# The compressed branch's softmax on ScalarE head by head, and one head in four of the full-length branch weighed by VectorE

## What is computed

```python
s = jnp.einsum('bqgrd,bngd->bgrqn', q, kc) * scale + tbl[:, :, t5_bucket(dist)]
p_cmp = masked_softmax(s, dist >= 0)            # compressed branch: at most 63 columns
...
p = masked_softmax(s, (dist >= 0)[:, :, None])  # selected blocks: with 1024 tokens, all 16 blocks
...
p = masked_softmax(s, mask)                     # sliding window of 512
...
return gates[:, :, 0] * o_cmp + gates[:, :, 1] * o_slc + gates[:, :, 2] * o_win
```

## Time and profile before

| | us |
|---|---|
| median of 3 runs | 1511.42 (1508.46 to 1513.57) |
| the profiled execution | 1514.9 |
| its span, first to last instruction | 1513.1 |
| PE busy | 1422.4 (94%) |
| DVE busy | 792.3 (52%) |
| ACT busy | 488.1 (32%) |
| POOL busy | 452.5 (30%) |

### The profile page before, as it was taken

How to read it: one execution, slowest core, us unless ns; L and a number is a source line. 1 busy time by engine, 2 the same in 40 slices (tenths; PEclk the granted TensorE clock), 3 DMA queues, 4 the chain that set the end, 5 groups by cost and what they waited for, 6 DMA issues and landing times.

```text
span 1513.1 us, 22442 instructions
## 1 busy us (share of the span) xinstructions
PE 1422.4 (94%) x8759; PEld 1330.7 (88%) x8759; DVE 792.3 (52%) x1541; ACT 488.1 (32%) x984; POOL 452.5 (30%) x453
## 2 busy tenths in 40 slices
PE   6999999888788888899999999999999999999997
PEld 6999988656566666699999999999999999999996
DVE  5489933226889997522433343435243434435257
ACT  5122124236776776422321121111112111112123
POOL 1113201466888889134210001010101101010105
PEclk9999999999999999899999999999999999999998
DMA  7731114943111102133110202112020202021112
GB/s 201 190 69 42 46 31 125 288 115 88 43 28 29 27 3 43 29 85 99 56 42 18 71 23 66 44 41 72 16 74 15 74 18 67 26 62 50 35 49 115
DMA packets 165817, 99.00 MB, mean 65 GB/s; under 512 B 35650, under 2 KB 160537, under 8 KB 165633
## 3 DMA queue, kind: packets, MB, share of 16 engines
q1 hardware_dynamic: 163217, 88.71, 21.4%
q0 software_dynamic: 2496, 8.88, 2.2%
HBM read 78.33 MB, written 13.19 MB: 60 GB/s over the span
## 4 chain that ended last, share of the span: by engine, by line
PE 78%; DVE 11%; ACT 4%; issue 4%; DMA 1%; SPq 1%; POOL 0%; POOLq 0%; DVEq 0%; ACTq 0%
PE psA L1077 16%; PE psB L1077 16%; PE psC L1077 16%; PE psA L790 4%; PE psB L790 4%; PE psC L790 4%; PE psC L739 3%; DVE small L1835 2%; PE psA L1106 2%; DVE probL L1886 2%; PE psB L1106 2%; PE psC L1106 2%; PE psD L739 1%; DVE ybuf L1670 1%; ACT probH L1324 1%
## 5 line engine op out<-in xcount | busy, mean ns | idle before, releaser
L2224 POOL TENSOR_TENSOR hid<-hid,rstdB 128x352 f32<-128x352 f32 x66 | 74.8, 1164 | 628.9 <-ACT hid L1507 628.9
L1446 ACT CAST wH<-wraw 128x1024 fp32r<-128x1024 f32 (+1 forms) x132 | 86.8, 658 | 259.7 <-PE psC L1077 178.0
L1904 DVE TENSOR_TENSOR wL<-wraw,wH 128x1024 fp32r<-128x1024 f32 (+1 forms) x132 | 107.2, 813 | 37.3 <-ACT wH L1446 37.2
L2201 POOL TENSOR_SCALAR wide<-wide,small 128x128 f32<-128x128 f32 (+7 forms) x64 | 109.3, 1725 | 24.0 <-DVE small L1878 23.8
L1077 PE MATMUL psA<-gH,wH 128*128 128x352 f32 x352 | 113.9, 324 | 0.1
L1077 PE MATMUL psB<-gH,wH 128*128 128x352 f32 x352 | 113.7, 323 | 0.0
L1077 PE MATMUL psC<-gH,wH 128*128 128x352 f32 x352 | 113.5, 322 | 0.0
L1077 PE MATMUL psA<-gH,wL 128*128 128x352 f32 x352 | 113.0, 321 | 0.0
L1077 PE MATMUL psA<-gL,wH 128*128 128x352 f32 x352 | 112.9, 321 | 0.0
L1077 PE MATMUL psB<-gH,wL 128*128 128x352 f32 x352 | 112.9, 321 | 0.0
L1077 PE MATMUL psC<-gL,wH 128*128 128x352 f32 x352 | 112.9, 321 | 0.0
(11 more groups left out here) (430 smaller groups left out, 4120.6 us busy)
## 6 DMA issues: line engine op xcount, KB each, us to landing
wraw<-in_w_gu SPq DMA_DIRECT2D x44, 512.0 KB
wraw<-in_w_down SPq DMA_DIRECT2D x80, 128.0 KB
zraw<-in_w_in SPq DMA_DIRECT2D x12, 512.0 KB
xa<-in_x_prompt SPq DMA_DIRECT2D x8, 512.0 KB, 8.7
pages<-in_cache_cmp_kv SPq DMA_DIRECT2D x32, 128.0 KB, 2.5
qS<-qH SPq DMA_DIRECT2D x32, 128.0 KB, 2.4
qS<-qL SPq DMA_DIRECT2D x32, 128.0 KB, 2.4
xs<-in_x_prompt SPq DMA_DIRECT2D x8, 512.0 KB, 3.8
```

What stands on the lines that cost most here:

```text
L1446: sc_.copy(wH[:, par, 0:nk, :], wraw[:, par, 0:nk, :]).then_inc(s["wH_done"], 1)
L1904: dve.tensor_tensor(wL[:, par, 0:nk, :], wraw[:, par, 0:nk, :], wH[:, par, 0:nk, :].bitcast(F32), ALU.subtract).then_inc(s["wL_done"], 1)
L2201: pool.tensor_scalar(p, p, precs[q % 4][:, r:r + 1], None, ALU.mult).then_inc(s["scaled"], 1)
L2224: pool.tensor_tensor(hid[:, n, :], hid[:, n, :], rstdB[:, c0:c0 + cw], ALU.mult).then_inc(s["up_scaled"], 1)
```

## The change

In the compressed branch VectorE no longer subtracts the maximum: it only reduces it (negated, into `cmax`). ScalarE makes eight exponentials in place of one, each with that head's `cmax` column as bias and its sum into a column of `csum`. VectorE forms 1/sum times gate (`c_weights`), and ScalarE multiplies the eight heads by their weights with eight copies (`c_scale`, now in ScalarE's program, at step (q+1, 1), ahead of the tiles of that step).

In the full-length branch (br 1) head 3 of each group is multiplied by its weight on VectorE (`weigh_head`), at step (q+2, 0), behind that step's bias and maximum, and GpSimd leaves it out. TensorE waits for both counts. Three semaphores are gone: `tri_in` is merged into `posr_in`, `gain2_in` into `gain_in`.

```diff
@@ module
+def weighed(q):
+
+    by_dve = sum(DG.index(n) <= q for n, _ in BY_DVE)
+    return GQ * (q + 1) - by_dve, by_dve
+
+BY_DVE = [(n, GQ - 1) for n in DG if GROUPS[n][2] == 1]
@@ semaphores and loads
-            sp.dma_start(tri[:, :], A["c_tri"]).then_inc(s["tri_in"], 16)
+            sp.dma_start(tri[:, :], A["c_tri"]).then_inc(s["posr_in"], 16)
...
-                        sp.dma_start(gain2[:, :], A["norm2"][0].rearrange("(k p) -> p k", p=P)).then_inc(s["gain2_in"], 16)
+                        sp.dma_start(gain2[:, :], A["norm2"][0].rearrange("(k p) -> p k", p=P)).then_inc(s["gain_in"], 16)
...
-            pe.wait_ge(s["posr_in"], 64)
+            pe.wait_ge(s["posr_in"], 80)
@@ TensorE
-                            pe.wait_ge(s["scaled"], GQ * (DENSE[n] + 1))
+                            pe.wait_ge(s["scaled"], weighed(DENSE[n])[0])
+                            pe.wait_ge(s["scaled_d"], weighed(DENSE[n])[1])
@@ ScalarE
-                    sc_.activation(pcmp[:, :, :, 0:w].rearrange("p r g n -> p (r g) n"),
-                                   p_scores(n, r).rearrange("p (x n) -> p x n", n=HD)[:, :, 0:w], ACT.Exp
-                                   ).then_inc(s["exp_done"], 1)
+                    for r_ in range(GQ):
+                        for g in range(KVH):
+                            k = KVH * r_ + g
+                            op = sc_.activation(pcmp[:, r_, g, 0:w], p_scores(n, r)[:, HD * k:HD * k + w], ACT.Exp,
+                                                bias=cmax[:, k:k + 1], accum_out=csum[:, k:k + 1])
+                    op.then_inc(s["exp_done"], 1)
...
+            def c_scale(n):
+
+                i, w = GROUPS[n][0], g_width(n)
+                sc_.wait_ge(s["cmp_rec"], i + 1)
+                for r in range(GQ):
+                    for g in range(KVH):
+                        k = KVH * r + g
+                        op = sc_.activation(pcmp[:, r, g, 0:w], pcmp[:, r, g, 0:w], ACT.Copy, scale=crec[:, k:k + 1])
+                op.then_inc(s["cmp_scaled"], 1)
...
-            for _, _, jobs, tiles in steps():
+            for q, r, jobs, tiles in steps():
...
+                if r == 1 and q and rider(q - 1) is not None:
+                    c_scale(rider(q - 1))
@@ VectorE
-                link2(dve.tensor_reduce(cmax, flat, AX, ALU.max, negate=True))
-                dve.tensor_tensor(flat, flat, cmax[:, :, None].to_broadcast([P, 2 * GQ, w]), ALU.add).then_inc(s["score_in"], 1)
-
-            def c_scale(n):
-
-                i, w = GROUPS[n][0], g_width(n)
-                flat = pcmp[:, :, :, 0:w].rearrange("p r g n -> p (r g) n")
+                dve.tensor_reduce(cmax, flat, AX, ALU.max, negate=True).then_inc(s["score_in"], 1)
+
+            def c_weights(n):
+
+                i = GROUPS[n][0]
                 dve.wait_ge(s["exp_done"], NSJ + LASTJOB[n] + 1)
-                link2(dve.tensor_reduce(csum, flat, AX, ALU.add))
+                if i:
+                    dve.wait_ge(s["cmp_scaled"], i)
                 link2(dve.reciprocal(crec, csum))
...
-                link2(dve.tensor_tensor(rg, rg, gate, ALU.mult))
-                dve.tensor_tensor(flat, flat, crec[:, :, None].to_broadcast([P, 2 * GQ, w]), ALU.mult
-                                  ).then_inc(s["cmp_scaled"], 1)
+                dve.tensor_tensor(rg, rg, gate, ALU.mult).then_inc(s["cmp_rec"], 1)
...
+            def weigh_head(n, r):
+
+                p = prob(n, r)[:, 0:g_width(n)]
+                dve.tensor_scalar(p, p, precs[DENSE[n] % 4][:, r:r + 1], None, ALU.mult).then_inc(s["scaled_d"], 1)
...
                     if head == 0:
                         group_weights(DG[old])
+                    if (DG[old], head) in BY_DVE:
+                        weigh_head(DG[old], head)
                 if r == 3 and rider(q) is not None:
-                    c_scale(rider(q))
+                    c_weights(rider(q))
@@ GpSimd
                 for r in range(GQ):
+                    if (n, r) in BY_DVE:
+                        continue
                     p = prob(n, r)[:, 0:g_width(n)]
                     pool.tensor_scalar(p, p, precs[q % 4][:, r:r + 1], None, ALU.mult).then_inc(s["scaled"], 1)
```

More of the change, by code:

```diff
@@ L452, in build @@
             "const_in pack_in table_in table4_in gain_in x_in0 x_in1 x_in2 x_in3 x_in4 x_in5 x_in6 x_in7 x_in8 state_in z_in0 z_in1 z_in2 chan_in poolw_in "
-            "tri_in table_mm table_ev stab_mm stab_ev fvec_ev fvec_out btab_in tsel_done prep "
+            "table_mm table_ev stab_mm stab_ev fvec_ev fvec_out btab_in tsel_done prep "
             "sq_done ms_done rstd_done xn_done turn_x evac_xa evac_xd state_turn state_ev "
@@ L458, in build @@
             "late_zero turn_fill turn_drain page_in0 page_in1 page_in2 page_in3 cmpw_in0 cmpw_in1 cmpw_in2 cmpw_used cmp_half cmp_sum cmp_ev posr_in "
-            "gate_mm gate_ev qbd_done score_mm score_in exp_done sum_read cmp_scaled turn_drain_d probT_used keys_used out_done rec_done scaled pl_done o_half o_ev v_pad split_done k_in q_in0 q_in1 q_in2 prob_zero "
+            "gate_mm gate_ev qbd_done score_mm score_in exp_done sum_read cmp_rec cmp_scaled turn_drain_d probT_used keys_used out_done rec_done scaled scaled_d pl_done o_half o_ev v_pad split_done k_in q_in0 q_in1 q_in2 prob_zero "
             "x2_in0 x2_in1 x_pad mixH_done mixL_done raw_in0 raw_in1 wH_done wL_done unit_mm third_mm out_ev rest_ev "
-            "acc_done moment_mm sd_done inv_done t_done silu_done up_scaled hid_done aH_done aL_done y_add gain2_in "
+            "acc_done moment_mm sd_done inv_done t_done silu_done up_scaled hid_done aH_done aL_done y_add "
             "lraw_in0 lraw_in1 lH_done lL_done last_mm y_last back_turn x_add sq_y accf_done ms3 rstd3 y_done_d y_done_a y_out").split()
@@ L707, in load_gu @@
                     sp.wait_ge(s["rest_ev"], 3 * KD)
-                    sp.dma_start(gB[:, :], A["final_norm"][None, :].to_broadcast([P, D])).then_inc(s["gain2_in"], 16)
+                    sp.dma_start(gB[:, :], A["final_norm"][None, :].to_broadcast([P, D])).then_inc(s["gain_in"], 16)
                 for x in range(2 * FT):
@@ L1479, in _ @@
                     sc_.wait_ge(s["mixL_done"], KD)
-                    sc_.wait_ge(s["gain2_in"], 16)
+                    sc_.wait_ge(s["gain_in"], 32)
                 for n, (at, w) in enumerate(tchunks):
@@ L1779, in _ @@
             dve.wait_ge(s["btab_in"], 16)
-            dve.wait_ge(s["tri_in"], 16)
+            dve.wait_ge(s["posr_in"], 80)
             def biased_max(job, sc, w, adds):
@@ L1873, in group_weights @@
                 if q >= 4:
-                    dve.wait_ge(s["scaled"], GQ * (q - 3))
+                    dve.wait_ge(s["scaled"], weighed(q - 4)[0])
+                    dve.wait_ge(s["scaled_d"], weighed(q - 4)[1])
                 dve.reciprocal(rc, psums[q % 4]).then_inc(s["sum_read"], 1)
@@ L1933, in _ @@
                                   ).then_inc(s["mixL_done"], 1)
-            dve.wait_ge(s["gain2_in"], 16)
+            dve.wait_ge(s["gain_in"], 32)
             for m in range(KD):
@@ L2025, in last_scale @@
                                       ).then_inc(s["y_done_d"], 1)
-            dve.wait_ge(s["gain2_in"], 32)
+            dve.wait_ge(s["gain_in"], 48)
             for q, turns in last_steps():
@@ L2189, in out_sum @@
                 u = 2 * i + g
-                pool.wait_ge(s["scaled"], GQ * min(2 * u + 6, len(DG)))
+                pool.wait_ge(s["scaled"], weighed(min(2 * u + 6, len(DG)) - 1)[0])
                 pool.wait_ge(s["o_half"], u + 1)
```

## The result

Median of 14 runs each: 1517.47 us after (1515.03 to 1520.93) against 1513.19 before (1508.46 to 1515.55). The ratio is 1.0033, with a 95% interval of 1.0022 to 1.0043: by it the change makes the kernel slower by 5.0 us (3.3 to 6.5); the two medians alone lie 4.3 us apart. The forecast said slower, by 11 us.

A forecast was written before the change was run, and what follows sets the result against it. VectorE was taken to set the pace in the prompt's attention, ScalarE close behind. Bursts +12.5, sum and scaling -6.7, weighings +6.9, GpSimd holds +1.5 gave +14.2 us; less a fifth, +11: 1522 us, range 1508 to 1534.

The forecast's parts named there:

- The bursts in early tiles: Tiles 0 to 3: ScalarE's added exponentials and copies delay the casts VectorE needs, costing VectorE 7.6 us.
- The bursts in late tiles: Tiles 4 to 7: the same runs of ScalarE exponentials and copies make VectorE late by 4.9 us.
- What leaves VectorE: Compressed branch: sum and scaling gone, 6.7 us saved; the subtraction's 3.0 us taken into the bursts instead.
- The weighings: Full-length branch: sixteen in-place multiplications of one head by its weight, new on VectorE, costing 6.9 us.
- a fifth: Taken off the summed +14.2 us, as a late VectorE waits less at its next wait; leaves +11 us.
- Held by GpSimd: VectorE's new weighings wait for running GpSimd instructions: 3.5 us left in 8 of 15 groups, 1.5 counted.
- The signs that were to be seen: Attention, 353 to 593 us: expected changes in ScalarE's busy time, VectorE's cast waits, GpSimd's weighings and the last maximum.
- absorbed: Rival, attention: VectorE catches up the bursts fully, only its own account counts: -1.3 us, 1510; chance 0.22.
- faster: Rival, attention: weighings and exponentials fall into VectorE's waits: -6.7 us, 1505; chance 0.11; faster as an outcome 0.13.
- within: Outcome for the whole kernel: change of no more than about 0.3% (4.5 us), given 0.26.
- The tail: After the last score at 593 us: set by w_out's transfer, then transposes and casts; after 622 us shifted as a whole.
- ring of three engines: Attention: TensorE's scores, VectorE's maximum, ScalarE's exponential, transpose, ScalarE's cast, VectorE's rest; added ScalarE work can reach VectorE.

The follow-up runs named there:

- E1: The whole change without VectorE's weighings (GpSimd weighs all heads again), timed against the kernel before: ratio 1.0021, +3.2 us.
- E2: The kernel before with only the weighing of head 3 of each full-length group moved to VectorE: ratio 1.0018, +2.7 us.
- E11: The kernel before with two idle one-column copies added on VectorE behind each of the 128 maxima: ratio 1.0063, +9.5 us.
- E10: The kernel before with one idle one-column copy added on ScalarE behind each of the 128 full-length exponentials: ratio 1.0011, +1.7 us.
- E6: The whole change for query tiles 4 to 7 only, the rest as in the kernel before: ratio 0.9987 against it, -2.0 us.
- E12: The kernel before with only the eight exponentials and their sums on ScalarE, in tiles 4 to 7; VectorE scales, GpSimd weighs all: ratio 0.9993, -1.1 us.
- E8: The whole change with ScalarE's eight copies per tile spread as four pairs over four steps: ratio 1.0032 against the kernel before, +4.8 us.

## Why the prediction was right in sign and too large

**The bursts in early tiles: right in sum.** The forecast had 7.6 us for tiles 0 to 3. E1's early stretch grew by 6.3 us while VectorE shed 3.4. What that shed time is worth isn't measured beside the bursts: nothing, if it goes as with the weighings there, or 1.7 at the half that E2 and E11 show without them. So the bursts cost 6.3 to 8.0 us (an estimate from these traces). At tile 2 the forecast expected 2.1 us of burst and VectorE's rest 1.36 late; the trace shows 2.05, and 1.55 us of idle before the rest. Tile by tile it fits less well: from the first mark of a tile to that of the next, tiles 0 to 3 of E1 are 1.3, 2.4, 0.6 and 1.4 us longer than before, and the forecast's bursts were 1.0, 2.9, 2.1 and 1.6. That the sum came out so near owes something to luck. ScalarE's added time, forecast 27.4, is 12.7 + 13.2 = 25.9 us over the stretches.

**The bursts in late tiles: too large.** Forecast 4.9. E1's late stretch shrank by 1.7 while VectorE shed 9.3, worth between nothing and 4.7: the bursts cost 3.0 at the most. E10 agrees in direction: late, more ScalarE work costs nothing. At tile 6 the forecast had VectorE 0.5 late by the exponentials, and the trace shows 0.39 us of idle at 530.02, so this one place came near. Where the rest of the late bursts is taken up isn't shown.

**What leaves VectorE: a term too small, at a price too high.** L1859, L1864 and L1852 were counted as 9.7 us, 3.0 of them held back. E1 shows 12.7 us less; the rest, some 3 us, is the weight multiplications, which got shorter (in the whole change L1878 to L1899 8.3 to 6.6 us, L1863 to L1885 2.6 to 1.4; in E1 3.3 us together); the forecast had L1878's waits for GpSimd stay.

**The weighings: the time right, the price wrong.** Forecast 6.9 us of VectorE's time; the difference between the whole change and E1 is 2.15 + 4.86 = 7.0 us. A column costs 0.52 ns, as assumed (0.28 us at 128 columns, 0.75 at 1024). But the sum counted each at full price less a fifth. Alone it costs half (E2: 3.7 of 7.1), and beside the bursts almost nothing (0.2 in the traces), since the bursts make VectorE wait for the cast and the weighing stands in that wait: of E1's 26.1 us of waits for the cast 19.7 are left. This is the mis-sized term that mattered most: 6.9 and 1.5 in the sum, 0.2 in the traces.

**Held by GpSimd: seen, and smaller.** The forecast had 8 of 15 weighings meet a GpSimd instruction with 3.5 us left in all, and took 1.5. Eight of the sixteen did meet one; beside their undisturbed times they lost 1.0 us together (below). "Some near 2 us" was wrong: the longest took 1.06.

**The step that failed** is the last of the sum, adding terms of two engines one to one and taking off a fifth. The early half came as forecast: 7.6 bursts, less 3.3, plus 2.4 of weighings and 0.4 held, less a fifth, makes 5.7; 6.3 was measured. As the weighings in it cost nothing there, this closeness too is in part luck. The late half had 5.7 by the same working and measured -1.5. The signs that were to be seen: ScalarE +27 (+21.5 in the fixed window), wait for the cast over 18 (18.4), GpSimd's wide weighings 48 (48), the last maximum near 604 (596.9), VectorE's idle not above 27 would have been wrong (37). The forecast describes the early tiles. The late ones lie between two rivals: by their own terms for this half, "absorbed" gives +0.8 us and "faster" -3.4.

**How near the number was.** +5.0 us is the lower end of the forecast's own +5 to +20, and less than half of the 11. The 1522 us stood beside a median of 1511.4 from three runs; with fourteen the median before is 1513.2. Of the 6.1 us from 1511.4 to the measured 1517.5, 1.8 are that shift and not the change.

**Two slips in the working.** The weights given for "within" and "faster" come to 0.23 and 0.15 and not to 0.26 and 0.13. And the rows give 0.25 us for an exponential without its columns (0.35 less 0.10), not 0.243, 0.3 us more over all 64. Neither changes the forecast.

**The tail** was forecast as a pure shift. Of the 3.75 us by which the last mark came later it kept 3.05 at the first matmul of the output projection (628.75 against 625.70).

**A version that beats both:** E6, 0.13% faster than before (0.02 to 0.24%), and 0.46% than the whole change by the two ratios; the gain is small, and the simpler E12 lies within its interval.

## What to carry to other kernels

Work out the price of an engine's microsecond, stage by stage, before adding terms: in this ring of three engines the traces show half of it on VectorE and less on ScalarE, and two added costs can fall into the same wait. A kernel with some hundred idle instructions added to one engine is a way to measure that price, if its trace and its timed runs agree (for ScalarE here they do, for VectorE they don't). A change whose cost depends on width or on slack should be read in parts (here early and late tiles), as a small net can be a loss and a gain that each deserve their own answer. Spreading a burst over steps gained nothing here, where the engine ran these steps without a gap; whether it helps where there are gaps wasn't run.

## What the runs showed of the hardware

A VectorE in-place multiplication in SBUF does wait for a running GpSimd `TENSOR_SCALAR`, but not always until that instruction has ended. Four of the sixteen weighings of after, the GpSimd instructions that ran beside the first three, and then one pair from E2:

```profile
511.49 0.79 DVE L1905 TENSOR_SCALAR wide<-wide,small 128x768 f32<-128x768 f32 x1
...
554.22 1.06 DVE L1905 TENSOR_SCALAR wide<-wide,small 128x896 f32<-128x896 f32 x1
...
598.08 0.88 DVE L1905 TENSOR_SCALAR wide<-wide,small 128x1024 f32<-128x1024 f32 x1
...
578.82 0.75 DVE L1905 TENSOR_SCALAR wide<-wide,small 128x1024 f32<-128x1024 f32 x1
...
509.67 2.20 POOL L2231 TENSOR_SCALAR wide<-wide,small 128x768 f32<-128x768 f32 x1
...
552.28 2.52 POOL L2231 TENSOR_SCALAR wide<-wide,small 128x896 f32<-128x896 f32 x1
...
597.31 2.84 POOL L2231 TENSOR_SCALAR wide<-wide,small 128x1024 f32<-128x1024 f32 x1
```

```profile
595.35 1.00 DVE L1904 TENSOR_SCALAR wide<-wide,small 128x1024 f32<-128x1024 f32 x1
...
594.68 2.85 POOL L2230 TENSOR_SCALAR wide<-wide,small 128x1024 f32<-128x1024 f32 x1
```

Undisturbed, a weighing takes 0.28 us at 128 columns, 0.62 at 768, 0.68 at 896 and 0.75 at 1024. The one at 511.49 ended 0.41 us behind GpSimd's instruction, the one at 554.22 0.48 behind it, which is what 768 and 896 columns cost at 0.52 ns each (0.40 and 0.47). Three more, of 256, 384 and 512 columns, ended 0.14, 0.21 and 0.28 behind theirs, by the same pace 0.13, 0.20 and 0.27. So these five waited for the end and then did their own work, as at the earlier trace rows. They agree with the rule of the Trainium skill ("SBUF — State Buffer", section "Who interferes with whom") that a VectorE instruction in a two-port mode and a GpSimd instruction exclude each other for the whole instruction, whichever came first (which mode the weighing ran in no trace shows). A sixth, at 368.00, met only the last 0.18 us and lost nothing.

The other two don't agree with "the whole instruction": the one at 598.08 (1024 columns) and one of 128 columns at 358.53 ended 1.19 and 0.14 us before the GpSimd instruction that they began in. The wide one recurs in E2 (the pair above), E6 and E8. It began 0.66 to 0.81 us after GpSimd's start, took 0.85 to 1.00, and ended 1.66 us after that start in all four. So here VectorE waited too, but was let in part-way, some 1.1 us after GpSimd's start (my estimate: 1.66 less 1024 columns at 0.52 ns). What opens that place isn't shown, and the profile's times on GpSimd are rough. In sum the sixteen lost 1.0 us of VectorE's time.

Short ScalarE instructions cost nearly the same whatever their width: eight exponentials of 23 columns with a bias pointer and an accumulator read repeat every 0.25 us, of 55 columns every 0.28; copies of 15 columns with a scale pointer every 0.20 (two in 0.49 to 0.51 us in E8). A one-column copy between two others is recorded with 184 ns on ScalarE and added some 0.08 us of busy time (9.8 us for 128), as its neighbours overlap it.
